# A hybrid attention and delta-rule block on one Trainium2 core: the attention stage in another order

## The reference

```
h = rms_norm(x, norm_w)
qa,ka,va,za, qb,kb,vb,zb, ab,bb, gate = split(h @ w_in)
# branch A: differential attention, 4 heads, each two maps of 64 channels, values of 128
q, k = rms_norm per 64 channels (with gains)
mask[q, k] = key chunk <= query chunk            # chunks of 64 tokens
p = softmax(q0 k0 / 8 masked) - lam * softmax(q1 k1 / 8 masked)
ya = rms_norm(p @ v, gain per head) * (1 - lambda_init) * silu(za)
# branch B: short convolution, gated delta rule in chunks of 64, rms_norm, silu(zb)
merged = sigmoid(gate_a) * (ya @ w_up_da) + sigmoid(gate_b) * (yb @ w_up_gdn)
out = x + merged @ w_out
```

## Time and profile before

| | |
|---|---|
| median of 3 runs | 1021.48 us |
| profiled execution | 1021.89 us |
| its span, first to last instruction | 1020.2 us |
| TensorE busy | 983.0 us (96%) |
| VectorE, ScalarE, GpSimd busy | 546.7, 357.7, 285.3 us |
| stage C in the trace, last fill step before it to the first up-projection | 523.75 to 837.41 us |

### The profile page before, as it was taken

One profiled execution on the slowest core, in us unless ns is written; L12 is line 12 of the kernel. 1 busy time (PEld: TensorE's weight loads), 2 busy tenths in 40 slices (PEclk: granted clock), 3 DMA queues, 4 the chain that ended last, 5 costly groups with the idle time before them and its releaser, 6 DMA issues. The chain is left out here.

```text
span 1020.2 us, 15922 instructions
## 1 busy us (share of the span) xinstructions
PE 983.0 (96%) x5355; PEld 809.7 (79%) x5355; DVE 546.7 (54%) x1394; ACT 357.7 (35%) x773; POOL 285.3 (28%) x239
## 2 busy tenths in 40 slices
PE   7999999999999999999999999999998979999998
PEld 6888888887888888888877777777776658887887
DVE  4677776656555664566344555555555556554012
ACT  5332333433332333333235444444544542211100
POOL 4242332543223223221242223223214112222221
PEclk8999999999999999999999999999999989999999
DMA  6022122121121122021111101101110012223342
GB/s 213 22 51 51 41 51 51 33 62 54 52 62 53 32 63 63 21 73 42 32 31 32 31 21 31 31 21 31 28 24 22 21 56 73 98 72 124 124 132 105
DMA packets 70893, 56.92 MB, mean 56 GB/s; under 512 B 3298, under 2 KB 61884, under 8 KB 70844
## 3 DMA queue, kind: packets, MB, share of 16 engines
q1 hardware_dynamic: 69552, 54.15, 18.4%
q10 hardware_dynamic: 1292, 2.14, 0.7%
HBM read 48.40 MB, written 7.88 MB: 55 GB/s over the span
## 5 line engine op out<-in xcount | busy, mean ns | idle before, releaser
L1132 PE MATMUL PS<-h_hi,w_hi 128*128 128x512 f32 x784 | 318.7, 406 | 1.8 <-DVE h_lo L1537 1.4
L606 POOL TENSOR_TENSOR w_lo<-w_raw,w_hi 128x512 fp32r<-128x512 f32 x130 | 183.9, 1415 | 476.0 <-ACT w_hi L748 475.9
L1136 PE MATMUL PS<-h_hi,w_lo 128*128 128x512 f32 x784 | 314.5, 401 | 0.0
L1134 PE MATMUL PS<-h_lo,w_hi 128*128 128x512 f32 x784 | 312.2, 398 | 0.0
L1132 PEld LDWEIGHTS PS<-h_hi,w_hi 128*128 128x128 f32 x784 | 148.2, 189 | 31.0 <-DVE h_lo L1537 2.0
L1136 PEld LDWEIGHTS PS<-h_hi,w_lo 128*128 128x128 f32 x784 | 147.9, 189 | 27.7
L1134 PEld LDWEIGHTS PS<-h_lo,w_hi 128*128 128x128 f32 x784 | 148.0, 189 | 25.5
L748 ACT ACTIVATE w_hi<-w_raw 128x512 fp32r<-128x512 f32 x130 | 81.6, 629 | 196.3 <-PE PS L1136 131.5
L716 POOL TENSOR_TENSOR at_s<-at_s,neg_half 128x1 f32<-128x1 f32 x32 | 17.6, 550 | 168.7 <-DVE at_s L1909 168.7
L1041 ACT ACTIVATE prob<-PS,nm,r_qk 128x128 f32<-128x128 f32 (+7 forms) x64 | 52.6, 827 | 18.1 <-DVE nm L1878 17.7
L1596 DVE SCALAR_TENSOR_TENSOR acc<-pre,cw,acc 128x1024 f32<-128x1024 f32 x36 | 57.2, 1588 | 1.3
(11 more groups left out here) (243 smaller groups left out, 1456.8 us busy)
## 6 DMA issues: line engine op xcount, KB each, us to landing
w_raw<-in_w_in SPq DMA_DIRECT2D x98, 256.0 KB, 2.8
x_in<-in_x SPq DMA_DIRECT2D x8, 512.0 KB, 8.1
w_raw<-in_w_out SPq DMA_DIRECT2D x16, 256.0 KB, 3.2
x_res<-in_x SPq DMA_DIRECT2D x8, 512.0 KB, 4.2
out<-out_sb SPq DMA_DIRECT2D x16, 256.0 KB, 2.1
gate_dram<-gate_st SPq DMA_DIRECT2D x7, 512.0 KB, 2.9
gate_a<-gate_dram SPq DMA_DIRECT2D x7, 512.0 KB, 4.1
grow<-g_dram ACTq DMA_DIRECT2D x8, 256.0 KB, 3.3
```

Source lines behind the costliest of these rows:

```text
L606: pool.tensor_tensor(w_lo[:, b, :], w_raw[:, b, :], w_hi[:, b, :].bitcast(F32), ALU.subtract)\
L1132: pe.matmul(dst, w, hi, start=first, stop=False)
L1134: pe.matmul(dst, w, lo, start=False, stop=False)
L1136: mm = pe.matmul(dst, lo_w, hi, start=False, stop=last)
```

## The change

Stage C is written anew, without hardware loops, over 32 pairs of head and tile (`s`), and the parts around it are fitted:

- Tiles go in falling order: t = 7 (1024 keys) first, t = 0 last.
- The next head's k, v and q are prepared inside tiles 3, 2 and 1 of the current head (`k_transposes`, `k_back`, `q_transposes`, `v_transposes` in two halves, each at the place "prep"). q_hi, q_lo, k_hi, k_lo and r_qk have two buffers. For head 0 the K transposes are put in stage B at step 790 of its fill; `k_back(0)` is the first thing in stage C.
- The fill is one run of 15 tiles (C_FILL) with one table of places (C_STEPS), `fill_to` on TensorE and `keep_up_c` on ScalarE and GpSimd. The first 44 steps belong to head 0's start.
- The output norm works on half a head: ScalarE copies each tile's output to o_raw, and for four tiles together there are one square, one chain on VectorE (`batch_mean`), one power of four columns, one scaling (`batch_norm`), four transposes (`batch_transposes`) and one y (`batch_y`).
- The mask product is fp32r with 64 output rows instead of float32 with 128.
- On ScalarE the exponentials of tile s+1 come ahead of the copy of tile s's transposed probabilities. v_st, v_tok and k_tok fall away: v is transposed in place in zv, and scaled keys go to n_sq.
- y_hi and y_lo are two tensors each. Branch B's are made in tiles 4 to 1 of the last head, branch A's after it, the half of the late tokens first. Stage D takes branch B first and its halves as (1, 0). The gate of block 7 of branch A goes through DRAM like the others.

The core of the diff:

```diff
-            link(pool.memset(mask_lhs[:, :], 0.0))
-            link(pool.memset(mask_lhs[0:1, 0:CHUNK], 1.0))
+            link(pool.memset(neg_rows[:, :].bitcast(F32), NEG))
+            for m in range(2): ...
-        C_START, C_TILE = (24, 16, 8), (6, 5, 4, 3)
-        C_START_LAST, C_TILE_LAST = (20, 14, 8), (4, 4, 3, 2)
+        C_K_FIRST, C_V_FIRST, C_Q_FIRST, C_S_FIRST, C_FIRST = 790, 0, 18, 22, 44
+        C_STEPS = ({7: (9, 6, 5), 6: (6, 7, 7), 5: (6, 7, 7), 4: (6, 7, 7), 3: (6, 6, 16), 2: (6, 6, 16), 1: (6, 6, 16), 0: (6, 6, 16)},
+                   {7: (9, 5, 3), 6: (6, 6, 5), 5: (6, 6, 5), 4: (6, 6, 5), 3: (3, 4, 1), 2: (3, 4, 1), 1: (3, 4, 1), 0: (3, 4, 1)})
+        for s in range(N_S):
+            h, t = head_tile(s)
+            steps = C_STEPS[h == HEADS - 1][t]
+            C_PLACE[s, "scores"], C_PLACE[s, "out"] = n, n + 3
+            C_PLACE[s, "T"] = n + steps[0]
+            C_PLACE[s, "PV"] = n + steps[0] + steps[1]
+            C_PLACE[s, "prep"] = C_PLACE[s, "PV"] + min(2, steps[2])
+            n += sum(steps)
 # GpSimd
             keep_up(48 * B_TILES)
...
+            norm_pow(0, 1)
+            keep_up_c(C_Q_FIRST)
+            norm_pow(0, 0)
+            for s in range(N_S):
+                h, t = head_tile(s)
+                keep_up_c(C_PLACE[s, "scores"])
+                if t == NT - 1 and h > 0:
+                    batch_pow(2 * h - 1)
+                if t == 3:
+                    batch_pow(2 * h)
+                if t == 2 and h + 1 < HEADS:
+                    norm_pow(h + 1, 1)
+                if t == 0 and h + 1 < HEADS:
+                    norm_pow(h + 1, 0)
+                keep_up_c(C_PLACE[s, "prep"])
+            keep_up_c(48 * C_TILES)
+            batch_pow(2 * HEADS - 1)
 # ScalarE
+            for s in range(N_S):
+                h, t = head_tile(s)
+                keep_up_c(C_PLACE[s, "scores"])
+                if s + 1 < N_S:
+                    exps(s + 1)
+                keep_up_c(C_PLACE[s, "T"])
+                take_probs(s)
+                keep_up_c(C_PLACE[s, "PV"])
+                take_out(s)
+                if t % 4 == 0:
+                    batch_squares(2 * h + (t < 4))
+                if t == 6:
+                    z_tanh(h)
+                if h + 1 < HEADS:
+                    keep_up_c(C_PLACE[s, "prep"])
+                    if t == 3:
+                        square_k(h + 1)
+                        take_v(h + 1, 0)
...
+                elif 1 <= t <= 4:
...
+                    round_y(0, 4 - t, slice(0, SEQ))
 # TensorE
+            k_back(0)
+            v_transposes(0, 0)
+            fill_to(C_Q_FIRST)
+            q_transposes(0)
+            v_transposes(0, 1)
+            fill_to(C_S_FIRST)
+            scores(0)
+            for s in range(N_S):
+                h, t = head_tile(s)
+                fill_to(C_PLACE[s, "scores"])
+                if s + 1 < N_S:
+                    scores(s + 1)
+                if t == NT - 1 and h > 0:
+                    fill_to(C_PLACE[s, "out"])
+                    batch_transposes(2 * h - 1)
+                fill_to(C_PLACE[s, "T"])
+                if t == 2:
+                    batch_transposes(2 * h)
+                prob_transposes(s)
+                fill_to(C_PLACE[s, "PV"])
+                weighted_values(s)
+                if h + 1 < HEADS and t in (3, 2, 1):
+                    fill_to(C_PLACE[s, "prep"])
...
+            whole(fill)
+            batch_transposes(2 * HEADS - 1)
 # VectorE
+            def batch_mean(b):
+                first = A_TILES[b % 2][0]
+                dve.reciprocal(a_l[:, :], l_sum[:, first:first + 4, 0]).then_inc(c_oms.sem, 1)
+                dve.wait_ge(c_osq.sem, c_osq.at(b))
+                dve.reduce_sum(a_ss[:, :], a_sq[:, :, :], AX.X).then_inc(c_oms.sem, 1)
...
+            def batch_norm(b):
+                dve.wait_ge(c_opow.sem, c_opow.at(b))
+                dve.tensor_tensor(a_f[:, :], a_r[:, :], a_l[:, :], ALU.mult).then_inc(c_on.sem, 1)
+                dve.wait_ge(c_on.sem, c_on.at(b, 1))
+                o = o_raw[:, b % 2, :, :]
+                dve.tensor_tensor(o, o, a_f[:, :].unsqueeze(2).broadcast_to([P, 4, P]), ALU.mult).then_inc(c_on.sem, 1)
...
+            for s in range(N_S):
+                h, t = head_tile(s)
+                more = h + 1 < HEADS
+                if t == NT - 1 and h > 0:
+                    batch_mean(2 * h - 1)
+                if s + 1 < N_S:
+                    maxima(s + 1)
+                if t == NT - 1 and h > 0:
+                    batch_norm(2 * h - 1)
+                    batch_y(2 * h - 1)
+                if t == 3:
+                    batch_mean(2 * h)
+                if t == 2 and more:
+                    scaled_keys(h + 1)
+                if t == 1 and more:
+                    rest_of_k(h + 1)
+                if s + 1 < N_S:
+                    combine(s + 1)
+                if t == 5:
+                    z_silu_of(h)
+                if t == 4 and more:
+                    rest_of_q(h + 1)
+                if t == 3:
+                    batch_norm(2 * h)
+                    if more:
+                        head_norms(h + 1, 1)
+                if t == 2:
+                    batch_y(2 * h)
+                if t == 1 and more:
+                    head_norms(h + 1, 0)
+                if 1 <= t <= 4 and not more:
+                    rest_of_y(0, 4 - t, slice(0, SEQ), 4 - t)
+            batch_mean(2 * HEADS - 1)
+            batch_norm(2 * HEADS - 1)
+            batch_y(2 * HEADS - 1)
```

More of the change, by code:

```diff
@@ L407, in b_events @@
             return events
-        C_START, C_TILE = (24, 16, 8), (6, 5, 4, 3)
-        C_START_LAST, C_TILE_LAST = (20, 14, 8), (4, 4, 3, 2)
[L412 to L426, removed]
-            events = []
-            for g in range(tiles):
-                events += [(48 * g + 24, 48 * g + 48, ("split", g, 0)), (48 * g + 36, 48 * g + 48, ("take", g, 0)),
-                           (48 * g + 48, 48 * g + 60, ("take", g, 1)), (48 * g + 48, 48 * g + 72, ("split", g, 1))]
-            order = {}
-            for can, need, what in events:
-                at = next(i for i, p in enumerate(places) if can <= p[3])
-                if places[at][0] == "scores" and need >= places[at + 1][2] + SLACK:
-                    at += 1
-                kind, t, behind, ahead = places[at]
-                assert need >= behind or need > 48 * tiles, (what, kind, t)
-                order.setdefault((kind, t), []).append(what)
-            return order
@@ L1228, in each_head, with c_fill_tiles, k_transposes @@
                     last.then_inc(signal.sem, 1)
+            def c_fill_tiles():
+                for g in range(G_C, G_C + C_TILES):
+                    yield from projection(g, g)
+            def k_transposes(h):
+                pe.wait_ge(proj_out.sem, proj_out.at(qk_tile(1, h)))
+                for t in range(NT):
+                    mm = pe.transpose(PS[:, 3 + 2 * (t // 4), (t % 4) * P:(t % 4 + 1) * P],
+                                      qk_raw[:, 1, t * P:(t + 1) * P], ident[:, :])
+                mm.then_inc(c_kT1.sem, 1)
             def fill_tiles():
@@ L1378, in out_transpose @@
-            def out_transpose(st):
-                pe.wait_ge(c_on.sem, c_on.at(st))
-                pe.transpose(PS[:, 7, 0:P], on_a[:, :], ident[:, :]).then_inc(c_oT.sem, 1)
-            def head(h, last):
-                fill, start, tile = next_tiles(h, last), *((C_START_LAST, C_TILE_LAST) if last else (C_START, C_TILE))
-                take(fill, start[0])
-                pe.wait_ge(c_y.sem, c_y.at(h * NT - 1))
-                pe.wait_ge(c_v.sem, c_v.at(h))
-                for t in range(NT):
-                    mm = pe.transpose(PS[:, 6 + t // 4, (t % 4) * P:(t % 4 + 1) * P], v_st[:, t * P:(t + 1) * P], ident[:, :])
-                mm.then_inc(c_vT.sem, 1)
-                take(fill, start[1])
+            done[0], fill = 0, c_fill_tiles()
@@ L1445, in head @@
-                whole(fill)
-                if not last:
-                    qk_transposes(h + 1)
-                out_transpose(h * NT + (NT - 1))
-            def next_tiles(h, last):
-                for i in range(LAST_TILES if last else 4):
-                    yield from projection(h * 4 + (G_C + i), h * 4 + (G_C + i))
-            pe.wait_ge(proj_out.sem, proj_out.at(G_QK + 1))
-            qk_transposes(0)
-            with pe.Fori(0, HEADS - 1) as h:
-                head(h, False)
-            head(HEADS - 1, True)
```

690 lines of the change are left out of this document (388 added, 302 removed).

## The result

The changed kernel takes 1026.44 us (median of 5), the kernel before 1021.48: ratio 1.0054, 95% interval 1.0032 to 1.0076. It is slower by half a per cent, as forecast (1026.7); the interval lies clear of 1. The profiled execution is 1027.67 us with a span of 1025.9.

What follows compares the result with a forecast made beforehand. TensorE, busy 96% of the span, was taken as the bound: its work plus its holes. The terms -35 - 8 + 0.6 + 43.3 + 4.3 = +5.2 us on 1021.89 gave a stated 1026.7 us, range 1012 to 1036.

Steps and rivals of the forecast that it cites:

- old waits removed: Attention stage: TensorE's waits in the old order all go, 35 us saved, with 30 as the other end.
- mask: Mask products of 32 tiles: fp32r with 64 columns takes 0.11 instead of 0.36 us a tile, 8.0 us saved.
- entry: Stage's start: TensorE waits 7.1 to 7.3 us for scaled keys, then 1.9 in head 0's q chain, +9.0 us.
- copy of the probabilities, heads 0 to 2: First three heads' tiles: the copy of transposed probabilities follows the next scores and exponentials, so TensorE waits, +10.2 us.
- scaling of the half head: Output norm of the second half head: scaling stands behind t=6's maxima on VectorE, 3.06 us three times, +9.2 us.
- last head: Last head's tiles: few fill steps, late copies, then y rounding and subtraction ahead of exponentials and maxima, +9.6 us.
- exit: After the last weighted values: one fill step left to cover copy, weight split, power and scaling, +5.3 us.
- clock: TensorE's half clock behind the entry's hole, in the last head and at half head borders, +4.3 us, bounds 0 and 8.
- The first: Rival: new waits don't bind, fill hides copies and batch norms; 1003 us, 1014 with half gone; chance 0.23, whole or half.
- The second: Rival: waits are as forecast but TensorE's clock stays up; 1022.5 us, no change; chance 0.13.
- The third: Rival: mask products of 64 columns are no cheaper, 8 us more, 1035 us; chance 0.22 together with the fourth.
- the fourth: Rival: old waits were 30 us, not 35, or ports are contended; 1032 us; chance 0.22 together with the third.

Runs made afterwards that it cites:

- e1_entry: Changed kernel with, at head 0's entry, k's power ahead of the last weight split (GpSimd) and scaled keys ahead of q's split (VectorE): 1019.58 us, ratio 0.9987.
- e2_norm_first: Changed kernel with the previous half head's scaling ahead of the next tile's maxima on VectorE, in tile 7 of heads 1 to 3: 1019.09 us, ratio 0.9981.
- e6_exit: Changed kernel with power ahead of last split, 24 stage D products ahead of output transposes, four y_lo pieces ahead of y: 1025.17 us, ratio 1.0038.
- e3_copy_first: Changed kernel with the copy of a tile's transposed probabilities ahead of the next tile's exponentials on ScalarE: 1014.59 us, ratio 0.9932.
- e7_last_head: Changed kernel with the subtraction for branch B's y_lo one tile later on VectorE in the last head: 1023.71 us, ratio 1.0025.
- all four kernels: Kernel before (1021.48 us), changed kernel (1026.44), kernel before with only the new mask product (1018.47), changed kernel with the mask back in float32 (1035.07).
- both mask runs: Kernel before with only the fp32r, 64-row mask: 1018.47 us, ratio 0.9972; changed kernel with the mask back in float32: 1035.07 us, ratio 1.0128.

## Why the prediction was right

The sign, the places and the mechanism of the new waits were right, but for part of the last head's. That the size came out within 0.3 us of the median is in part luck: two errors of 6 to 7 us cancel, as shown below. The terms compare as follows; a measured hole is the distance between starts less the 0.23 of the step before it.

| term | predicted | measured |
|---|---|---|
| old waits removed | -35 | about -31, what is left over in the stage's sum |
| mask | -8.0 | -4.8 |
| before the border | +0.6 | +0.3 (border 1.2 us later, 0.9 of it the moved K transposes) |
| entry | +9.0 | +9.6 (7.95 and 1.70) |
| copy of the probabilities, heads 0 to 2 | +10.2 | +7.6 |
| scaling of the half head | +9.2 | +8.3 |
| last head | +9.6 | +6.4 |
| exit | +5.3 | +5.4 |
| clock | +4.3 | about +3 |
| sum | +5.2 | +4.8; +5.7 by the spans |

- **Entry, scaling, exit.** Each is one chain in a fixed order behind one place, and each came within 1 us; e1_entry, e2_norm_first and e6_exit took each away, or nearly (the entry's 7.8 us to 2.2), by orders alone. The entry's first hole was 0.8 longer than I had it: the power took 3.88 us beside VectorE's split of q, where I had 2.9, and the weight split took 1.26 where I had 1.48.
- **Copy of the probabilities.** The mechanism is shown by e3_copy_first. The size was too large by 5.8 us over both rows of the table, and the 12.1 us of waits for probT lie under the 15 to 20 that I had named as a sign of being right: in head 0's first tile a wait for weights (0.25 us) came ahead and took part of it, and in the last head t=1 lost nothing, where I had 2.2. e7_last_head shows that only part of the cycle I had drawn for these tiles was what TensorE waited for. The stretch from 829.8 to 832.9, at half clock, lies just there, so TensorE came late itself; that this is the cause is argued, not shown.
- **Mask.** The term of 8.0 was mis-sized. The step that failed is that the 0.34 us fill step behind the mask would go back to 0.23. It stays at 0.34 in all four kernels, float32 or not, and behind transposes and weighted values the first fill step takes 0.31 to 0.32 as well. So a hand-over of 0.08 to 0.1 us is paid wherever fill follows other products, and no change of the mask's type could save it. By the Trainium skill's four passes (FP8 and Floating Point Precision, TensorE Precision Notes) I had 0.07 a tile for the product. The slot is 0.12 for 0.26, a ratio of 2.2 and not 4, so the row of the 128-column pair was the better guide.
- **Old waits.** The stage (525.22 to 842.56) is 3.9 us longer than before. With 37.8 us of new waits (0.4 of them for weights), 4.8 off for the mask, 0.9 off for the K transposes that moved ahead and 3 for the clock, 31 are left for the old ones. 35 was too much, the lower end of 30 nearer. Not all of the 31 are waits: with the output transposes in batches, fill follows other products 110 times in the stage instead of 135, and 25 hand-overs of 0.085 are about 2 us by estimate, a gain that the prediction left out, as it took all other products as no cheaper than before. Old waits and mask together were 7 us too hopeful for the change, the new waits 6 too dark, which cancels: the point forecast is nearer than its parts deserve.
- **Clock.** The fill steps at half clock lose 4.7 us against 2.1, and transposes add to it. Right in kind: half clock behind the entry, in the last head and behind the exit. In the profile of the changed kernel 21 fill steps run at it, before 10.
- **Rivals.** The first, that the new waits don't bind, is refuted by e1_entry, e2_norm_first and e3_copy_first, which each gained about what their wait had cost or more; it was right in part for the copies, which were hidden more than I had it. The second, that the clock stays up, fell with the 21 half-clock fill steps. The third, no gain from the mask, is refuted by both mask runs, though 3.2 of the 8 us weren't there. Of the fourth the premise was nearer than mine (old waits of 30), and the time of 1032 not, as the new waits were smaller.
- **Slips in the sums.** The addends of head 0's second chain give 9.8 and not 9.9, those of the last head 9.5 and not 9.6, those of the exit 5.4 and not 5.3; together they change the forecast by under 0.3 us.

What I hadn't seen at all is SP's queue: the gate that waits for the last y stands ahead of the next weights. I had written that it had 36 steps to land and stopped at the gate; what is queued behind it counts too.

## What to carry to other kernels

When an order is written out by hand for five queues, go through each place where TensorE waits and read the other queues backwards from it: whatever stands ahead of the awaited instruction is part of the hole, needed or not. Here the orders at five places (entry, norm, copy, exit, SP's queue), none of which changes the work, decided between 0.5% slower and 2.7% faster, and two more orders and two places made it 3.4%. And a hole that is removed can uncover a second one that it hid, so look again after each, at SP's queue too.

## What the runs showed of the hardware

- Some small VectorE instructions stretch beside GpSimd's weight split: at the exit one on 128x4 took 1.23 us (838.50), where in the seven other batches it took 0.17, and it ended when the split of 838.43 did. Three times another one on 128x4 (L2012) took 0.48 instead of 0.17 and ended with the split. Others of that size beside a split kept their 0.17 us (the reciprocal on 128x4, three times).
- A power of 16 columns on GpSimd took 3.88 us while VectorE split q, and 2.90 in the seven other cases of the changed kernel. That subtraction took 2.17 us beside weight split and power, and 1.23 in the other three heads. The Trainium skill (GPSIMD Engine Reference, Specifications, on the SBUF interfaces) says that the two engines share them, with contention for VectorE instructions in a 2-port perf mode or with two SBUF inputs; this case agrees (q_lo has two). Another doesn't: in the kernel before, VectorE's product of z (zv from z_th and zv, two SBUF inputs, 534.21) took 1.22 us beside a power that kept its 2.90; the same product takes 1.22 in the changed kernel too, beside a weight split or without.
- The clock doesn't answer one hole in one way: after the 2.5 us hole at 703.7 in the changed kernel fill steps ran at half clock, after the one of the same length at 627.6 none did. In e1_entry, where the stage runs 7 us earlier, it is the other way round: half clock after the hole at 620.0, none after that at 698.9.
- The shorter mask product was worth 4.8 and 4.5 us of slots in the two kernels, and 2.9 and 7.4 us of time, by the holes and the clock around it.
- A full-width fill step behind another kind of product takes 0.31 to 0.34 us instead of 0.23, in the four kernels of the mask comparison; so each group of small products between fill steps costs 0.08 to 0.1 us besides its own time.
